# Squaring the hidden layer twice: ScalarE for the high half, VectorE for the low half, without the skew

## The reference, cut to what matters

```
h = _rms_norm(x, norm_mlp[i]) * (1.0 + sc2) + sh2
x = x + g2 * (jnp.square(jax.nn.relu(h @ mlp_w1[i])) @ mlp_w2[i])
```

## Time and profile before

| what | value |
|---|---|
| median of 3 runs | 2726.83 us (2725.86 to 2728.61) |
| the profiled execution, its own time | 2724.42 us |
| its span, first to last instruction | 2722.7 us |
| mean granted TensorE clock | 0.972 |
| TensorE matmul busy | 2548.3 us (94%) |
| VectorE busy | 1460.5 us (54%) |
| ScalarE busy | 600.3 us (22%) |
| GpSimd busy | 605.9 us (22%) |
| one middle chunk of the first layer's MLP | 56.5 us |

### The profile page before, as it was taken

The page is one execution under the profiler, slowest core; times in us unless marked ns, Lnnn a source line. Parts: engine busy times, 40 slices in busy tenths (PEclk is TensorE's granted clock), DMA queues, the critical chain, the costliest instruction groups (busy, mean ns, idle before and its releaser), DMA issues.

```text
span 2722.7 us, 36898 instructions
## 1 busy us (share of the span) xinstructions
PE 2548.3 (94%) x14158; PEld 2203.5 (81%) x14158; DVE 1460.5 (54%) x2485; ACT 600.3 (22%) x968; POOL 605.9 (22%) x267
## 2 busy tenths in 40 slices
PE   7899999979879999999999995679999999999996
PEld 3878899968768888888888884458888888888885
DVE  6635832274674565555655558884434443444346
ACT  3311231152221111111111114441112112211113
POOL 6125421164212111121211214011121112121213
PEclk9999999999989999999999997889999999999998
DMA  7324433372121212111121110001010101110001
GB/s 242 133 78 155 134 123 112 128 274 90 32 78 55 69 54 92 54 56 68 54 92 54 61 63 31 0 16 47 31 46 31 46 31 44 33 46 31 31 31 78
DMA packets 126117, 198.91 MB, mean 73 GB/s; under 512 B 4404, under 2 KB 102488, under 8 KB 125656
## 3 DMA queue, kind: packets, MB, share of 16 engines
q1 hardware_dynamic: 123072, 188.23, 20.4%
q10 hardware_dynamic: 2968, 9.63, 1.1%
HBM read 166.91 MB, written 26.74 MB: 71 GB/s over the span
## 4 chain that ended last, share of the span: by engine, by line
PE 83%; DVE 8%; issue 3%; POOL 2%; DMA 2%; ACT 1%; ACTq 0%; SPq 0%; DVEq 0%; POOLq 0%
PE bank L286 78%; PE bank L1259 1%; DVE prow L1198 1%; PE bank L1289 1%; DVE hL L932 1%; POOL acc L778 1%; DMA ada_st_in<-in_ada_w_dram 1%; POOL ringL L767 1%; DVE hs L925 1%; DVE acc L887 1%; PE bank L1326 1%; DVE yT L1245 1%; DVE ada_acc_in L961 0%; DVE relu L1144 0%; PE bank L1515 0%
## 5 line engine op out<-in xcount | busy, mean ns | idle before, releaser
L286 PE MATMUL bank<-hH,ringH 128*128 128x512 f32 (+1 forms) x2064 | 746.8, 362 | 74.4 <-DVE hL L1186 38.2
L767 POOL TENSOR_TENSOR ringL<-stage,ringH 128x2048 fp32r<-128x2048 f32 x83 | 397.3, 4787 | 1831.3 <-ACT ringH L496 1831.3
L286 PE MATMUL bank<-hL,ringH 128*128 128x512 f32 (+1 forms) x2064 | 737.7, 357 | 0.0
L286 PE MATMUL bank<-hH,ringL 128*128 128x512 f32 (+1 forms) x2064 | 737.5, 357 | 0.0
L969 DVE SCALAR_TENSOR_TENSOR X<-bank,mod,X 128x512 f32<-128x512 f32 (+1 forms) x792 | 516.9, 661 | 356.9 <-PE bank L286 352.7
L286 PE MATMUL bank<-midH,ringH 128*128 128x512 f32 (+1 forms) x1536 | 546.1, 356 | 7.5 <-DVE X L969 6.5
L286 PE MATMUL bank<-midL,ringH 128*128 128x512 f32 (+1 forms) x1536 | 544.5, 355 | 0.0
L286 PE MATMUL bank<-midH,ringL 128*128 128x512 f32 (+1 forms) x1536 | 544.2, 354 | 0.0
L286 PEld LDWEIGHTS bank<-hH,ringH 128*128 128x128 f32 x2064 | 396.2, 192 | 141.0 <-issue 51.7
L1144 DVE TENSOR_TENSOR relu<-relu 128x512 f32<-128x512 f32 (+1 forms) x192 | 149.4, 778 | 572.0 <-ACT relu L698 572.0
L286 PEld LDWEIGHTS bank<-hH,ringL 128*128 128x128 f32 x2064 | 395.8, 192 | 55.8
(11 more groups left out here) (137 smaller groups left out, 1964.8 us busy)
## 6 DMA issues: line engine op xcount, KB each, us to landing
stage<-in_mlp_w_dram SPq DMA_DIRECT2D x64, 1024.0 KB, 5.3
ada_st_mlp<-in_ada_w_dram SPq DMA_DIRECT2D x18, 1536.0 KB, 8.3
stage<-in_ev_w_in_dram SPq DMA_DIRECT2D x14, 1024.0 KB, 5.1
ada_st_in<-in_ada_w_dram SPq DMA_DIRECT2D x8, 1536.0 KB, 9.6
ada<-in_ada_w_dram SPq DMA_DIRECT2D x8, 1024.0 KB, 13.5
x_spill<-X SPq DMA_DIRECT2D x1, 5120.0 KB, 18.7
gate_spill<-gate_st ACTq DMA_DIRECT2D x8, 640.0 KB, 3.3
gt<-gate_spill SPq DMA_DIRECT2D x20, 256.0 KB, 3.4
```

What stands on the lines that cost most here:

```text
L286: mm = nc.tensor.matmul(out, a, b, start=first and n == 0, stop=last and n == 2)
L767: nc.gpsimd.tensor_tensor(ringL[slot][:, :], stage[:, :], ringH[slot][:, :].bitcast(F32), ALU.subtract).then_inc(w_lo, 1)
```

## The change

ScalarE squares the relu while it rounds the high half, so it needs only the relu. VectorE still squares the same buffer in place, but behind ScalarE's read of it, and subtracts at once instead of one tile later.

```diff
 # ScalarE
             def hidden_hi(g):
-                act.wait_ge(sqr_ok[l], n0 + g + 1)
+                act.wait_ge(relu_ok[l], n0 + g + 1)
                 if g == 0:
                     after(act, m2_mm[l], GRP * ch)
-                act_ = nc.scalar.activation(midH[...], r_b[g % 3][...], ACT.Copy)
+                act_ = nc.scalar.activation(midH[...], r_b[g % 3][...], ACT.Square)
...
-                if g > 0:
-                    hidden_hi(g - 1)
-            hidden_hi(NTB * HT - 1)
+                hidden_hi(g)
 # VectorE
             def hidden_lo(g):
-                dve.wait_ge(mid_hi[l], n0 + g + 1)
+                dve.wait_ge(sqr_ok[l], n0 + g + 1)
...
             for g in range(NTB * HT):
-                dve.wait_ge(relu_ok[l], n0 + g + 1)
+                dve.wait_ge(mid_hi[l], n0 + g + 1)
                 r = r_b[g % 3][:, 0:TB[g // HT][1]]
                 V.tensor_tensor(r, r, r, ALU.mult).then_inc(sqr_ok[l], 1)
-                if g > 0:
-                    hidden_lo(g - 1)
+                hidden_lo(g)
                 if l == 0 and g >= 2:
                     ada_part(BATCHES_L0 + ch, 1, g - 2, 4)
-            hidden_lo(NTB * HT - 1)
```

More of the change, by code:

```diff
@@ L685, in hidden_hi @@
             def hidden_hi(g):
-                act.wait_ge(sqr_ok[l], n0 + g + 1)
+                act.wait_ge(relu_ok[l], n0 + g + 1)
                 if g == 0:
                     after(act, m2_mm[l], GRP * ch)
-                act_ = nc.scalar.activation(midH[:, g % HT, cols(g // HT)], r_b[g % 3][:, 0:TB[g // HT][1]], ACT.Copy)
+                act_ = nc.scalar.activation(midH[:, g % HT, cols(g // HT)], r_b[g % 3][:, 0:TB[g // HT][1]], ACT.Square)
                 act_.then_inc(mid_hi[l], 1)
```

## The result

The changed kernel takes 2833.89 us (median of 5 runs, 2833.31 to 2837.36) against 2725.86 (5 runs, 2723.63 to 2728.61) for the kernel before on the same chip. The ratio is 1.0398, 95% interval [1.0384, 1.0412]. The prediction's sum gave 2838.4, with a range of 2790 to 2862. The profiled execution takes 2833.31 us by its own time and 2831.6 by its span, 108.9 more than before's span; the mean granted clock is 0.957 (0.972).

A forecast was written before the change was run, and what follows sets the result against it. TensorE, busy 813 of 813 us in the middle chunks, was taken as the bound. 14 x (4.8 stall + 2.5 clock) = 102.2, plus 6.2, 3 and 0.2, gave 111.6 more: 2838.4 us, range 2790 to 2862.

The forecast's parts named there:

- The chain on VectorE and ScalarE, 0.41 per chunk: First MLP: VectorE's later square and hand-overs, less the low half moved ahead, start update 0 0.41 us later per chunk.
- The pass 1.3 us earlier, at 1185.63: Middle chunk: `hidden_hi` 5 needs only relu 5, so GpSimd's second `split_lo` starts at 1185.63 instead of 1186.92.
- Which instruction the pass holds: Middle chunks: `split_lo` gets in behind the first of four ada instructions and delays the other three; update 0 4.8 us later.
- GpSimd waits the run out (0.12): Rival, chance 0.12: `split_lo` waits until VectorE's run ends, only 0.41 per chunk stays; 2734.5, slower by 0.28%.
- The clock, 2.5 per middle chunk: After TensorE's stall in each middle chunk, matmuls run at the 1.2 GHz level, adding 2.5 us; bounds 0 and 3.4.
- First chunk 6.2, last 3: First MLP's end chunks: 6.2 us from VectorE's lateness, `split_lo` and clock; 3 from GpSimd's later additions, bounds 2 and 7.3.
- Second MLP 0.2: No `ada_part` there, so update 0 is never late; its first chunk's second product starts some 0.2 us later.
- The sum: All terms over both MLPs: 111.6 us added, 2836.0 for a profiled execution, 2838.4 as median.

The follow-up runs named there:

- Run 1: Changed kernel plus one ScalarE wait in the first MLP, putting GpSimd's second pass behind the chunk's ada instructions: 2736.15 us, ratio 1.0044.
- Run 2: Kernel before, with only the second `split_hi` moved ahead of the last `hidden_hi` in the first MLP, so GpSimd's pass starts earlier: 2820.64 us, ratio 1.0347.
- run 3: `skew_kept`: changed kernel, but VectorE subtracts one tile later, as before, so its run has no dependent neighbours: 2840.73 us, ratio 1.0423.
- moved_after: Changed kernel with 12 of 16 ada instructions of each first-MLP chunk but the last put one by one behind updates 4 to 15: 2730.16 us, ratio 1.0014.
- half_pass: Changed kernel with GpSimd's second pass in the first MLP's middle chunks cut to 1024 of 2048 columns: 2788.39 us, ratio 1.0229.

## Why the prediction was right, step by step

- **The chain on VectorE and ScalarE, 0.41 per chunk.** Run 1 isolates it: 0.43. It costs anything at all only because TensorE's slack was nil.
- **The pass 1.3 us earlier, at 1185.63.** Measured 1185.62 in before's time. Run 2 moves only the pass, by 1.45 us, and shows 95.9 of the 108.9 us.
- **Which instruction the pass holds.** Here the prediction was off by one: it let the first ada instruction run out (0.53 us) and had the pass start to work behind it. In the changed kernel the first one, started 0.02 us ahead of the pass, was itself held, for the 5.00 us shown above. Since the pass then also ends half a microsecond sooner, update 0 came at 1192.11, against 1192.1 predicted: the two errors are the same half microsecond and cancel. That the update was hit to 0.01 us is therefore luck; that it was hit to half a microsecond is not. The rule cited from the Trainium skill, page "SBUF — State Buffer", section "Who interferes with whom", foresees mutual exclusion, and the length agrees (5.00 = 4.56 + 0.44). Its "whoever issues first", which the page says of another kind of VectorE instruction and the prediction applied here, can't be read off the start times on record. The ada instruction started 0.02 us ahead of the pass and lost. In the kernel before, the last subtraction started 0.03 us behind the pass (1186.95 and 1186.92), and it was the pass that waited, as the prediction itself reads these rows. One fixed delay between recorded start and taking the ports does not give both, and what decides is not shown.
- **GpSimd waits the run out (0.12).** Did not come: 2734.5 against 2833.9 measured, and run 3 refutes the reading behind it.
- **The clock, 2.5 per middle chunk.** Right as a mechanism, 2.19 in size. The 2.5 came from taking half of the 4.8 to 5.3 us of the earlier trace rows; the spells turned out to have two lengths. Taking the 4.81 off what a chunk loses in all, 2.4 to 2.9 us go to one of 6.8 us (chunk 1: 7.34 - 4.81 = 2.53) and 1.4 to 1.6 to one of 3.4 (the chunk above: 6.18 - 4.81 = 1.37). Of the 14 middle chunks nine had the long spell and five the short one. That is 4.3 us in the sum, the largest mis-sized term.
- **First chunk 6.2, last 3.** Measured 5.2 and 3.2. In the first chunk the wait at tile 4 grew by 3.7 us (10.21 against 6.48) and the one in front of the second product by 1.2 (1.81 against 0.57). In the last chunk GpSimd's additions do end last, as argued from the earlier trace rows: TensorE loses 4.8 and some clock there too, but 3.2 remain at the second MLP.
- **Second MLP 0.2.** Measured 1.9, the one missed mechanism. In its first chunk TensorE stands for 6.6 us inside the first product in both kernels, until 1820.07 and 1927.04, and a spell of low clock of 6.8 us begins in that gap: at 1818.84 before, at 1923.03 after. Busy time by stretch, the kernel before up to the second product and behind its start:

```profile
1822.60:1829.00 6.40, 5.97 (x39) 5.80 (x38) 6.40 (x5) 2.52 (x6) 3.85 (x1) 0.76 0.17 41
1829.00:1834.00 5.00, 5.00 (x22) 4.16 (x23) 4.85 (x10) 3.95 (x6) 0.03 (x1) 1.00 0.44 157
```

The changed kernel, the same two stretches:

```profile
1929.90:1936.20 6.30, 4.37 (x38) 4.20 (x36) 6.23 (x5) 2.87 (x6) 3.55 (x1) 1.00 0.19 46
1936.20:1941.00 4.80, 4.80 (x14) 3.82 (x15) 4.66 (x10) 3.44 (x5) 0.00 (x0) 0.64 0.45 159
```

Before, the spell lasted until 1825.67, over the matmuls behind the gap. They ended later for it, which only used up time in which TensorE would have waited for the low halves (0.43 us of waiting were left). Afterwards the spell ended at 1929.86, earlier in the same matmuls. TensorE then waited 1.93 us, and a second spell, from 1936.68 on, fell on the start of the second product, where nothing covers it: 14 matmuls in 4.8 us, 1.6 us lost. The second product itself starts only 0.3 later, near the 0.2 predicted. In `skew_kept` and `moved_after` the wait was 1.90 and 1.94 us, and the same 1.6 were lost; in the other five runs it was at most 1.60, and nothing was. A spell's price hangs on where it falls, and the trace before could not tell that.

- **The sum.** 111.6 against 108.9: the clock -4.3, the first chunk -1.0, the second MLP +1.7, the last chunk +0.2, and 0.6 from the part ahead of the load at 769.05. These partly cancel; that the sum came within 3 us owes something to that.

What stays open: why GpSimd does wait out a run in three places ahead of the output projection. They are in every trace of this case, in the changed kernel too; VectorE's and GpSimd's timelines where the earlier trace rows are:

```profile
107.65 6.43 DVE L959 SCALAR_TENSOR_TENSOR ada_acc_in<-ada_st_in,sc,ada_acc_in 128x384 f32<-128x384 f32 x12
114.00 0.86 DVE L1001 BATCH_NORM_STATS2 vst<-vtok 128x6 f32<-128x128 f32 x4
```

```profile
111.99 6.58 POOL L765 TENSOR_TENSOR ringL<-stage,ringH 128x2048 fp32r<-128x2048 f32 x1 [28.03 <-ACT ringH L496]
```

The 6.58 are 4.58 and the 2.0 that remain of the run. It is neither the length of the run (run 3 has 14 unbroken) nor the pass (the same instruction and shape). Nor is it the pair of instructions: in the trace of the kernel before, the same pass and the same ada instructions also meet like this, VectorE's timeline, then GpSimd's:

```profile
278.96 8.08 DVE L961 SCALAR_TENSOR_TENSOR ada_acc_in<-ada_st_in,sc,ada_acc_in 128x384 f32<-128x384 f32 x3
```

```profile
281.17 4.92 POOL L767 TENSOR_TENSOR ringL<-stage,ringH 128x2048 fp32r<-128x2048 f32 x1
```

Here the pass, which follows another GpSimd instruction at once, holds the second of the three, which starts at 281.55, for 4.95 us. The prediction had only shorter GpSimd instructions as examples of a hold; this row would have shown the full-length one in advance. No experiment was made on the three places, and no cause is claimed.

## What to carry to other kernels

When an edit makes an engine's chain shorter, look for what it releases sooner, and lay that release over the timeline of the engine that it can hold: here a pass that nobody waited for came 1.3 us earlier and cost 4.4 us of TensorE in each of 14 chunks (4.81 less the 0.43 of the chain), and twelve instructions moved behind the updates took that cost away again. Price the held instruction at the whole length of the other engine's, and only where an instruction that frees TensorE's banks stands behind it; the same hold on square 0 cost nothing in the middle chunks. Add the clock once a gap reaches a few microseconds: a 4.6-us gap lost another 2.2 us on average, a 2.4-us gap another 1.0.

## What the runs showed of the hardware that was not expected

- The instruction that is held can be the one that started first: an ada instruction with a lead of 0.02 us was held for the whole pass (5.00 us), in `half_pass` likewise (1217.65 against 1217.67). With a lead of 0.13 us (`skew_kept`) it ran out, and the pass waited 0.33. A subtraction that started 0.03 us behind the pass (the kernel before) went first as well, and the pass took 4.93 us. The recorded starts alone do not say which of the two will wait.
- Between back-to-back VectorE instructions GpSimd gets in at a boundary, even in an unbroken run of 14 (`skew_kept`); yet in three places of every trace it waits 2 to 3.3 us until the run ends.
- Equal gaps of 2.4 us are followed by a spell of 1.2 GHz or not, 9 to 5 in 14 chunks; gaps of 4.57 always are (all 15 chunks of the changed kernel that have one), and the spells then have two lengths, 3.4 and 6.8 us.
